# Entering a feed-forward sublayer tile by tile: a decoder trunk on one core

## What is computed

```python
def _rmsnorm(x, g):
    xf = x.astype(jnp.float32)
    y = xf * lax.rsqrt(jnp.mean(xf * xf, axis=-1, keepdims=True) + EPS)
    return (y * g.astype(jnp.float32)).astype(x.dtype)

def _swiglu(x, w_up, w_down):
    g, u = jnp.split(x @ w_up, 2, axis=-1)
    return (jax.nn.silu(g) * u) @ w_down

# per layer
x = x + 0.5 * _rmsnorm(_swiglu(_rmsnorm(x, ng[0]), w_ffn_up[layer, 0], w_ffn_down[layer, 0]), ng[1])
# h = mixer(_rmsnorm(x, ng[2]))
x = x + _rmsnorm(h, ng[3])
x = x + 0.5 * _rmsnorm(_swiglu(_rmsnorm(x, ng[4]), w_ffn_up[layer, 1], w_ffn_down[layer, 1]), ng[5])
```

## Times and profile before

| | us |
|---|---|
| runs | 2861.23, 2863.91, 2865.24 |
| median | 2863.91 |
| profiled execution, its own time | 2865.3 |
| its span | 2863.4 |
| TensorE busy | 2707.9 (95% of the span) |
| VectorE busy | 1563.2 (55%) |
| ScalarE busy | 1138.6 (40%) |
| GpSimd busy | 257.1 (9%) |
| TensorE's granted clock, mean | 0.962 of full speed |

### The profile page before, as it was taken

One profiled execution on the slowest core, in us unless ns is written; L12 is line 12 of the kernel. 1 busy time (PEld: TensorE's weight loads), 2 busy tenths in 40 slices (PEclk: granted clock), 3 DMA queues, 4 the chain that ended last, 5 costly groups with the idle time before them and its releaser, 6 DMA issues.

```text
span 2863.4 us, 51802 instructions
## 1 busy us (share of the span) xinstructions
PE 2707.9 (95%) x22064; PEld 2531.5 (88%) x22064; DVE 1563.2 (55%) x1930; ACT 1138.6 (40%) x1487; POOL 257.1 (9%) x278
## 2 busy tenths in 40 slices
PE   8998998899999999989989989999999989998998
PEld 7997886799999886689989978789989978877998
DVE  5546744655565445465465453465465468446554
ACT  4334442434344344344343332344343344424432
POOL 1000003100100125010010000010010000031000
PEclk9999998899999999999999999999999999988999
DMA  6444431444544635444445452544445444314543
GB/s 198 157 151 131 148 95 39 135 161 147 160 162 145 191 110 165 142 138 163 145 158 167 146 170 83 165 143 163 145 159 168 145 127 146 109 31 125 172 143 99
DMA packets 415626, 404.19 MB, mean 141 GB/s; under 512 B 14787, under 2 KB 411951, under 8 KB 415087
## 3 DMA queue, kind: packets, MB, share of 16 engines
q1 hardware_dynamic: 411348, 397.39, 43.9%
q0 software_dynamic: 4096, 4.20, 0.5%
HBM read 385.16 MB, written 16.39 MB: 140 GB/s over the span
## 4 chain that ended last, share of the span: by engine, by line
PE 89%; DVE 8%; ACT 2%; issue 1%; DMA 0%; SPq 0%; ACTq 0%; DVEq 0%
PE psum L343 22%; PE psum L345 22%; PE psum L344 22%; DVE w_lo L325 2%; DVE x L508 1%; DVE y L506 1%; PE psum L1145 1%; PE psum L2560 1%; PE psum L359 1%; DVE xn_lo L443 1%; PE psum L1050 1%; PE psum L1067 1%; PE psum L936 1%; PE psum L1963 1%; PE psum L937 1%
## 5 line engine op out<-in xcount | busy, mean ns | idle before, releaser
L325 DVE TENSOR_TENSOR w_lo<-raw,w_hi 128x2048 fp32r<-128x2048 f32 (+4 forms) x374 | 764.3, 2044 | 562.4 <-ACT w_hi L318 562.3
L343 PE MATMUL psum<-xn_hi,w_hi 128*128 128x288 f32 x3296 | 986.4, 299 | 22.3 <-DVE w_lo L325 10.7
L344 PE MATMUL psum<-xn_lo,w_hi 128*128 128x288 f32 x3296 | 979.0, 297 | 0.0
L345 PE MATMUL psum<-xn_hi,w_lo 128*128 128x288 f32 x3296 | 975.6, 296 | 0.0
L318 ACT ACTIVATE w_hi<-raw 128x2048 fp32r<-128x2048 f32 (+4 forms) x374 | 639.1, 1709 | 786.5 <-PE psum L345 725.7
L343 PEld LDWEIGHTS psum<-xn_hi,w_hi 128*128 128x128 f32 x3296 | 624.2, 189 | 36.5 <-issue 15.3
L345 PEld LDWEIGHTS psum<-xn_hi,w_lo 128*128 128x128 f32 x3296 | 627.1, 190 | 0.0
L344 PEld LDWEIGHTS psum<-xn_lo,w_hi 128*128 128x128 f32 x3296 | 625.4, 190 | 0.0
L344 PE MATMUL psum<-h_lo,w_hi 128*128 128x288 f32 x1408 | 415.5, 295 | 0.0
L345 PE MATMUL psum<-h_hi,w_lo 128*128 128x288 f32 x1408 | 415.0, 295 | 0.0
L343 PE MATMUL psum<-h_hi,w_hi 128*128 128x288 f32 x1408 | 413.3, 294 | 0.0
(11 more groups left out here) (549 smaller groups left out, 3037.7 us busy)
## 6 DMA issues: line engine op xcount, KB each, us to landing
raw<-w_ffn_up SPq DMA_DIRECT2D x176, 1024.0 KB, 5.1
raw<-w_ffn_down SPq DMA_DIRECT2D x64, 768.0 KB, 4.4
raw<-w_ffn_down SPq DMA_DIRECT2D x64, 640.0 KB, 4.2
raw<-gdn_w_in SPq DMA_DIRECT2D x32, 1024.0 KB, 5.8
raw<-mlstm_w_in SPq DMA_DIRECT2D x12, 1024.0 KB, 5.4
raw<-gdn_w_out SPq DMA_DIRECT2D x8, 1024.0 KB, 7.0
raw<-cache_mla_latent SPq DMA_DIRECT2D x64, 128.0 KB, 2.4
a_split<-cache_mla_latent SPq DMA_DIRECT2D x64, 128.0 KB, 2.2
```

The lines of the kernel that those rows point to most:

```text
L325: dve.tensor_tensor(wview(w_lo[u % NSPL], u), wview(raw[u % NRAW], u), wview(w_hi[u % NSPL], u).bitcast(F32), ALU.subtract).then_inc(lo_re ...
L343: pe.matmul(out, wh[:, k, c], hi(k), start=st, stop=False)
L344: pe.matmul(out, wh[:, k, c], lo(k), start=False, stop=False)
L345: last = pe.matmul(out, wl[:, k, c], hi(k), start=False, stop=sp_)
```

## The change

- The chunks of the entry into a feed-forward sublayer become single feature tiles: eight updates of 288 columns instead of four of 576, ScalarE and VectorE signal xn_hi and xn_lo for each tile, and the counts x_ready, xhi_ready and xlo_ready are taken from a sum (entered) of each sublayer's number of cuts. Mixers keep their four chunks. The squares stay in pairs of tiles.
- The second unit of a feed-forward sublayer gets buffers of its own, second_hi and second_lo, in space that the mixers use too. Its split is done in the sublayer before, in front of the split of the next sublayer's first unit (act_second, dve_second); for n = 0 it stays in the entry. So that hi_ready and lo_ready count on as before, a copy of one element on each engine steps them in the entry after the second tile.
- TensorE's loop over the first two units has the feature tile outermost: 6 matmuls of the first unit, 6 of the second, for each of the eight tiles. Unit 0's last matmul is the 90th of 96; it was the 72nd. TensorE waits for both low parts before the first matmul.
- GpSimd's additions at an entry start when all four squares are there, not two. At the end of a sublayer they are as before.
- The input copies of n = 0 go by single tiles.

```diff
+        second_hi = at("second_hi", [P, UNIT], 2 * FC * T + 4 * T, F32R)
+        second_lo = at("second_lo", [P, UNIT], 2 * FC * T + 4 * T + UNIT, F32R)
...
+        def act_second(act, n):
+            u = second_of(n)
+            if u is not None:
+                act.wait_ge(raw_in[u % NRAW], 16 * (u // NRAW + 1))
+                act.activation(wview(second_hi, u), wview(raw[u % NRAW], u), ACT.Copy).then_inc(second_hi_ready, 1)
+
+        def dve_second(dve, n):
+            u = second_of(n)
+            if u is not None:
+                dve.wait_ge(second_hi_ready, nffn[n] + 1)
+                dve.tensor_tensor(wview(second_lo, u), wview(raw[u % NRAW], u), wview(second_hi, u).bitcast(F32),
+                                  ALU.subtract).then_inc(second_lo_ready, 1)
...
+        cuts = lambda n: KC if n < NSUB and subs[n][0] == "ffn" else H
+        entered = lambda n: sum(cuts(m) for m in range(n))
...
-            pool.wait_ge(sq_ready, H * q + 2)
+            pool.wait_ge(sq_ready, H * q + (2 if q % 2 else H))
...
-            for i in range(H):
-                act.wait_ge(x_ready, H * n + i + 1)
-                for k in (2 * i, 2 * i + 1):
-                    last = act.activation(xn_hi[:, k, :], x[:, k, :], ACT.Copy, scale=gain(l, g, k))
-                last.then_inc(xhi_ready, 1)
-                if i == 0:
-                    act_split(act, ubase[n] + 1)
-                else:
-                    if i == 1:
-                        act_square_x(act, n, 0)
-                    act_square_x(act, n, i)
+            for k in range(KC):
+                act.wait_ge(x_ready, entered(n) + k + 1)
+                act.activation(xn_hi[:, k, :], x[:, k, :], ACT.Copy, scale=gain(l, g, k)).then_inc(xhi_ready, 1)
+                if k == 1:
+                    if n == 0:
+                        act_second(act, 0)
+                    act.activation(eps_t[:, 2:3], eps_t[:, 0:1], ACT.Copy).then_inc(hi_ready, 1)
+                if k % 2 == 1:
+                    act_square_x(act, n, k // 2)
...
             def chunk(i):
-                c = slice(2 * i, 2 * i + 2)
-                dve.tensor_tensor(y[:, c, :], y[:, c, :], rr[:, 1:2, :].to_broadcast([P, 2, T]), ALU.mult).then_inc(t, 1)
-                dve.wait_ge(t, H * n + i + 1)
+                w_ = KC // cuts(n + 1)
+                c = slice(w_ * i, w_ * i + w_)
+                dve.tensor_tensor(y[:, c, :], y[:, c, :], rr[:, 1:2, :].to_broadcast([P, w_, T]), ALU.mult).then_inc(t, 1)
+                dve.wait_ge(t, entered(n + 1) - entered(1) + i + 1)
                 dve.tensor_tensor(x[:, c, :], x[:, c, :], y[:, c, :], ALU.add).then_inc(x_ready, 1)
...
+            pe.wait_ge(lo_ready, u0 + 1)
+            pe.wait_ge(second_lo_ready, nffn[n] + 1)
+            first_two = ((w_hi[u0 % NSPL], w_lo[u0 % NSPL]), (second_hi, second_lo))
+            for k in range(KC):
+                pe.wait_ge(xlo_ready, entered(n) + k + 1)
+                for g, (hi, lo) in enumerate(first_two):
+                    wh, wl = wview(hi, u0 + g), wview(lo, u0 + g)
+                    for m in range(2):
+                        out, c = psum[:, 4 + 2 * g + m, 0:T], slice(m * P, (m + 1) * P)
+                        pe.matmul(out, wh[:, k, c], xn_hi[:, k, :], start=k == 0, stop=False)
+                        pe.matmul(out, wh[:, k, c], xn_lo[:, k, :], start=False, stop=False)
+                        last = pe.matmul(out, wl[:, k, c], xn_hi[:, k, :], start=False, stop=k == KC - 1)
+                    if k == KC - 1:
                         last.then_inc(unit_used, 1)
...
             for i in range(H):
                 for q in range(DU):
+                    if i == H - 1 and q == DU - 1:
+                        act_second(act, n + 1)
                     if DU * i + q > 0:
                         act_split(act, u0 + 2 * PAIRS + DU * i + q + 1)
```

More of the change, by code:

```diff
@@ L412, in act_pre @@
             for i in range(H):
-                act.wait_ge(x_ready, H * n + i + 1)
+                act.wait_ge(x_ready, entered(n) + i + 1)
                 act_square_x(act, n, i)
@@ L425, in act_pre_ffn, with dve_low_x @@
                 act.wait_ge(vec_ready, 3)
-            for i in range(H):
-                act.wait_ge(x_ready, H * n + i + 1)
-                for k in (2 * i, 2 * i + 1):
-                    last = act.activation(xn_hi[:, k, :], x[:, k, :], ACT.Copy, scale=gain(l, g, k))
-                last.then_inc(xhi_ready, 1)
-                if i == 0:
-                    act_split(act, ubase[n] + 1)
-                else:
-                    if i == 1:
-                        act_square_x(act, n, 0)
-                    act_square_x(act, n, i)
-        def dve_low_x(dve, n, i):
-            l, g = subs[n][1], pre_gain(subs[n])
[L441 to L447, removed]
+            for k in range(KC):
[7 more added lines that the diff above has]
+                    act_square_x(act, n, k // 2)
+        def dve_low_x(dve, n, k):
+            l, g = subs[n][1], pre_gain(subs[n])
+            dve.wait_ge(xhi_ready, entered(n) + k + 1)
+            dve.scalar_tensor_tensor(out=xn_lo[:, k, :], in0=x[:, k, :], scalar=gain(l, g, k),
+                                     in1=xn_hi[:, k, :].bitcast(F32), op0=ALU.mult, op1=ALU.subtract).then_inc(xlo_ready, 1)
+            if k == 1:
+                if n == 0:
+                    dve_second(dve, 0)
+                dve.tensor_copy(eps_t[:, 3:4], eps_t[:, 0:1]).then_inc(lo_ready, 1)
         def dve_enter(dve, n, chunk):
             ffn = n < NSUB and subs[n][0] == "ffn"
-            for i in range(H + 1):
-                if i < H:
+            for i in range(cuts(n) + 1):
+                if i < cuts(n):
                     chunk(i)
@@ L467, in dve_pre @@
                     if i >= 2:
-                        dve.wait_ge(xlo_ready, H * n + i - 1)
+                        dve.wait_ge(xlo_ready, entered(n) + i - 1)
                     for k in (2 * i, 2 * i + 1):
@@ L473, in dve_pre @@
                 if i > 0:
-                    dve.wait_ge(xhi_ready, H * n + i)
+                    dve.wait_ge(xhi_ready, entered(n) + i)
                     dve.tensor_tensor(xn_lo[:, 2 * i - 2:2 * i, :], fbuf[:, (i - 1) % 2],
@@ L550, in pair @@
                             xn(xn_hi), xn(xn_lo), True, True, i=i, late=2 * n + 1 if jj == 1 and g == 0 else 0)
[L552 to L563, removed]
-                            last = pe.matmul(out, wl[:, k, c], xn_hi[:, k, :], start=False, stop=k == KC - 1)
-                    if k0 > 0:
+            pe.wait_ge(lo_ready, u0 + 1)
[11 more added lines that the diff above has]
+                    if k == KC - 1:
                         last.then_inc(unit_used, 1)
@@ L644, in dve_ffn @@
                 for q in range(DU):
+                    if i == H - 1 and q == DU - 1:
+                        dve_second(dve, n + 1)
                     if DU * i + q > 0:
@@ L2119, in dve_mlstm @@
             dve.memset(lvs[:, LC:LC + 1], 1.0).then_inc(sem("l_ones"), 1)
-            once(dve, "xlo_ready", H * (n + 1))
+            once(dve, "xlo_ready", entered(n + 1))
             dve.wait_ge(unit_used, u0 + 1)
@@ L2375, in pool_mla @@
                 if b == RSLOTS - 1:
-                    pool.wait_ge(xlo_ready, H * (n + 1))
+                    pool.wait_ge(xlo_ready, entered(n + 1))
                 elif b >= RSLOTS:
@@ L2751, in act_mla @@
             for i in range(H):
+                if i == H - 1:
+                    act_second(act, n + 1)
                 act_split(act, u0 + 7 + i + 1)
@@ L2946, in _ @@
                 PE[sub[0]](pe, n)
-            pe.wait_ge(x_ready, H * (NSUB + 1))
+            pe.wait_ge(x_ready, entered(NSUB + 1))
             for t, (cols, _, _) in enumerate(token_tiles):
@@ L2970, in _ @@
             dve.memset(eps_t[:, 1:2], P * EPS).then_inc(sem("eps_set"), 1)
-            for i in range(H):
-                dve.wait_ge(sem("x_turned"), 2 * i + 2)
-                dve.tensor_copy(x[:, 2 * i:2 * i + 2, :], psum[:, 2 * i:2 * i + 2, 0:T]).then_inc(x_ready, 1)
+            for k in range(KC):
+                dve.wait_ge(sem("x_turned"), k + 1)
+                dve.tensor_copy(x[:, k, :], psum[:, k, 0:T]).then_inc(x_ready, 1)
             dve.wait_ge(sem("vec_turned"), 1)
```

20 lines of the change are left out of this document (16 added, 4 removed).

## The result

The changed kernel takes **2882.8 us** (median of 4 runs, 2881.7 to 2884.9) beside 2862.8 for the kernel before in the same set (4 runs, 2861.2 to 2865.2): a ratio of **1.007, 95% interval 1.0053 to 1.0087**, 0.7% slower. The profiled execution took 2881.73 with a span of 2880.0, mean granted clock 0.958 (before: 2865.3, 2863.4 and 0.962).

What follows compares the result with a forecast made beforehand. TensorE bounds the kernel (89% of the chain), losing time at feed-forward entries; -1.5 (entries) + 4.5 (first sublayer) + 13.6 (clock behind second pause) = +16.6 us, median 2880.5 us. Own range 2871 to 2889, 2866 to 2890 with the short-pause case.

Steps and rivals of the forecast that it cites:

- Single tiles: Feed-forward entry: TensorE starts 2.38 us after t0 (VectorE's first update), 1.64 earlier, and doesn't wait for tiles.
- The moved split costs nothing in seven entries: Second unit's split, done in the sublayer before, fits into idle time there; cost nothing, uncovered up to 2.3 us an entry.
- The rival of an uncovered split: Sublayer before an entry: the moved split comes late, each entry pays up to 2.3 us, up to 2896 us; chance 0.06.
- GpSimd decides nothing in the new order: Entry: GpSimd starts about 10.8 us after t0, is done at 19.3 at most; the third unit comes after that.
- the 32 us that the rule alone gave: Seven entries: VectorE-GpSimd exclusion rule and rows alone give back contention (1.24 + 1.10) and split (2.20), 32 us; not adopted.
- The third unit 0.2 us earlier an entry: Seven entries: the third unit's first matmul starts 20.8 us after t0, 0.2 earlier each, 1.5 us in all.
- The first pause's clock: TensorE's idle before an entry's first matmul lowers its clock for 8 us behind: 1.9 us lost an entry.
- The second pause: Idle before the third unit grows from 0.72 to 3.1 us; lowered clock behind costs 1.7 us in eight entries, 13.6.
- The first sublayer: Its second split stays, ahead of TensorE's work: start 22.1 instead of 19.94, third unit 4.5 us later.
- The sum: Whole kernel: -1.5 + 4.5 + 13.6 = +16.6 us on the profiled execution, 2881.9; median 2880.5 us, 0.6% slower.
- that the second pause is short enough: Rival: clock stays at 1.00 behind the pause before the third unit in most entries, 2867 to 2870 us; chance 0.17.
- That neither pause costs: Rival: no clock lost behind an entry's first pause or the one before the third unit, 2853.5 us, faster; chance 0.07.

Runs made afterwards that it cites:

- run 1: Changed kernel with TensorE's old order for the last four tiles (unit 0's, then unit 1's), so 24 matmuls cover the split again: 2848.9 us, ratio 0.9954.
- run 4: Changed kernel with GpSimd's additions at an entry begun at two squares again, as before: 2880.4 us, ratio 1.006.
- run 3: Kernel before with only GpSimd's later start at an entry (fourth square): 2852.2 us, ratio 0.9961.
- Run 2: Changed kernel with 14 unread matmuls between the sum and the third unit, whose start stays where it was: 2868.3 us, ratio 1.0019.
- run 8: Changed kernel with 6 unread matmuls between the sum and the third unit, leaving a 2.32 us pause: 2872.6 us, ratio 1.0044.
- run 10: Changed kernel, old TensorE order for tiles 4 to 7 and throughout the first sublayer, sum moved behind 24 matmuls of unit 2, no fills: 2849.1 us, ratio 0.9954.
- run 6: Changed kernel with old TensorE order for the last four tiles and 22 unread matmuls before each entry but the first: 2858.4 us, ratio 0.9992.

## Why the prediction was right

Step by step:

- **Single tiles**: 2.38 after t0 was forecast and 2.38 measured in this entry, idle 3.43 for 3.4. VectorE's rows in sublayer 6 give the pair and the tile period, 1.29 us from one low part to the next, and the tiny copy (0.15) beside them:

```profile
1462.84 0.51 DVE L464 SCALAR_TENSOR_TENSOR xn_lo<-x,vec,xn_hi 128x288 fp32r<-128x288 f32 x1
1463.27 0.15 DVE L469 COPY eps_t<-eps_t 128x1 f32<-128x1 f32 x1
...
1464.19 0.52 DVE L464 SCALAR_TENSOR_TENSOR xn_lo<-x,vec,xn_hi 128x288 fp32r<-128x288 f32 x1
...
1465.48 0.51 DVE L464 SCALAR_TENSOR_TENSOR xn_lo<-x,vec,xn_hi 128x288 fp32r<-128x288 f32 x1
```

- **The moved split costs nothing in seven entries**: behind the mixer it was forecast to have VectorE done about 2 us before t0; the two splits end 2.0 us before t0 = 550.40:

```profile
543.51 2.71 DVE L367 TENSOR_TENSOR second_lo<-raw,second_hi 128x2048 fp32r<-128x2048 f32 x1 [0.87 <-ACT second_hi L360]
546.15 2.28 DVE L327 TENSOR_TENSOR w_lo<-raw,w_hi 128x2048 fp32r<-128x2048 f32 x1
548.35 0.93 DVE L513 TENSOR_SCALAR y<-psum,vec 128x288 f32<-128x288 f32 x2
550.40 0.46 DVE L529 TENSOR_TENSOR y<-y,rr 128x288 f32<-128x288 f32 x1 [1.12 <-ACT rr L426]
```

  L513 now follows right behind the split, but t0 waits for ScalarE's root: ScalarE's last square is 2.98 us ahead of t0 as before (547.42; 542.54 and 545.53 before). The rival of an uncovered split is refuted. The stretches without a mixer say the same: 201.1 us before and in run 1, which has the moved split and no lowered clock there.
- **GpSimd decides nothing in the new order**: it starts at 10.8 after t0 as forecast and is done at 16.3, nobody being beside it; the forecast's 19.3 was an upper bound. The margin is small: in this entry TensorE's last matmul before the sum starts at 16.5.

```profile
1470.66 1.43 POOL L396 TENSOR_TENSOR fbuf<-sq 128x576 f32<-128x576 f32 x1 [25.78 <-ACT sq L432]
1472.23 3.00 POOL L400 TENSOR_TENSOR fbuf<-fbuf,sq 128x576 f32<-128x576 f32 x2
1475.31 0.81 POOL L402 TENSOR_TENSOR fbuf<-fbuf 128x288 f32<-128x288 f32 x1
```

  Run 4 shows it from the other side. The rule of the Trainium skill that the prediction named (SBUF — State Buffer, Who interferes with whom) holds: in run 4, low part and addition start together and the low part takes 1.75 us, near the sum of 0.51 and 1.42, and in run 3 the contention is gone. Yet the 32 us that the rule alone gave, with the split, were not there: 9 in run 3, none in the changed kernel. The rule prices instructions, and the chain decides what is paid.
- **The third unit 0.2 us earlier an entry**: 146.0 over seven is 20.86 a piece, forecast 20.8; against before, 148.2, that is 0.3 earlier, -2.2 in all for a forecast of -1.5. The first pause's clock cost 2.2 us an entry (mean grant 0.73) where 1.9 was taken; sublayer 2, whose entry had been 21.86, gave 1.4 back.
- **The second pause**: 3.12 us, as forecast, in all eight entries. Its clock is the one term that was mis-sized: 18.5 us in the profiled execution for a forecast of 13.6, since four of the eight windows lie at 0.62 to 0.64, beyond the far end that was given (0.66, 2.7 us), and not at the 0.79 that was taken. That is 2.3 us an entry, just outside the 1.0 to 2.2 of the forecast's own range. Run 2, which removes only this, gives 14.5 by the medians, 1.8 an entry and inside. Between the two stand what differs from one execution to another, the grant outside the windows, and that a window at 0.79 counts 1.7 us where the stretch behind it grew by 1.5.
- **The first sublayer**: the start moved by 1.8 for 2.2 forecast, the third unit by 4.0 for 4.5.
- **The sum**: +16.6 forecast and +16.4 measured between the profiled executions. That they agree so well is partly luck: the entries alone give +20.3, and -3.7 came from the rest of the kernel, most of it from stretches with mixers, whose length differs by more than that between profiled executions. By the medians it is +20.0, and 2882.8 for 2880.5.

The rivals: that the second pause is short enough was refuted at 3.12 us, and run 8 shows how near it was: at 2.32 us it would have come true in half the entries. That neither pause costs was refuted in every window. What remains open is by what the two pauses of an entry are coupled (runs 4 and 8 show that they are), and what sets the grant in the mixers.

## What to carry to other kernels

A rotation of buffers ties the last reader of one buffer to the first reader of another: when a loop order is changed, count for each buffer how much work follows its last use, since that work is the cover for whatever refills it. Price a pause of TensorE twice, its length and the clock behind it; here they were some 19 (a remainder) and 14.5 us. A pause that can't be removed can be shortened by matmuls that nobody reads; look first at what TensorE will wait for next. And price a contention only where the slowed instruction is the one that the chain waits for: the same GpSimd edit was worth 9 us in one kernel and nothing in the other.

## What the runs showed of the hardware that was not expected

- The same pause in the same place can leave the clock or lower it: 2.32 us did each in four of eight entries (run 8). Pauses of 1.15 to 1.26 us never lowered it, nor did 1.65 and 1.73 (run 10) or one of 1.87 (run 1, sublayer 11), but 1.79 and 1.86 did in run 10, and 2.96 left it at 1.00 once (run 6); 3.12 us did in all eight. So between 1.79 and 2.96 us the length alone didn't decide here; in run 8 the grant behind the first pause told which entries were hit. The Trainium skill (TensorE: Matmul & The Clock Gate, HAM oscillation) tells of groups of matmuls that each start cold; the changed kernel's entries agree, with waits for VectorE: 39 to 49 matmuls in the windows behind both pauses where a window at 1.00 holds 60.
- A pause can be filled with matmuls whose result nobody reads: 14 of them, 2.24 us on the timeline, brought back 14.5 us over eight entries.
- TensorE sped up by a fill lost what it won in a wait of 2.96 us at the sum, and the clock with it (run 6).
- GpSimd suffers from VectorE's weight splits too: its addition of 128x288 took 0.81 us alone and 2.72 with a split beside it (run 6).
